# Early modulation: 27 of 64 weight chunks split into high and low parts, the other 37 left as they were

## The chip, the cores and the metric

One core of a Trainium2 chip runs the whole program. The metric is the device time of one execution in microseconds, from the first to the last instruction and what lies around them. Beside the timed runs there is one profiled execution, whose trace is what is read here.

## The reference

One layer of a streaming encoder runs over 512 prompt rows and 32 sample rows of width 2048. Two conditioning vectors (prompt and sample) give scales, shifts and gates for the rows:

```python
cs = jax.nn.silu(c)
mod = cs @ w_mod[li] + b_mod[li]              # w_mod is 2048 x 12288
sh_a, sc_a, gt_a, sh_f, sc_f, gt_f = [m[:, None, :] for m in jnp.split(mod, 6, axis=-1)]
h = rmsnorm(x, g_attn[li]) * (1.0 + sc_a) + sh_a
z = h @ w_in[li]
...                                           # two kinds of attention, w_out, a second norm
f, cnew = conv_ffn(h2, cstate, w_up[li], conv_w[li], conv_b[li], w_down[li])
```

Everything is float32. Before the first large product (`h @ w_in`) can run, the first third of `mod` must be known: the 4096 columns of `sh_a` and `sc_a`.

## The kernel before

**The early stage.** That first third is computed on TensorE with the two conditioning vectors as the stationary operand (two columns) and the weights of `w_mod` as the moving one. The weights come in 64 chunks, e0 to e63, of 128 partitions x 1024 values (512 KB). Eight chunks make a group (8 groups of 512 output columns); a chunk holds two blocks of 128 input rows by 512 columns, so there are two matmuls of 512 moving columns per chunk, in plain float32 (L1558). The profile shows each of them as two records.

**Buffers and the order of loads.** Four raw buffers `w_raw0` to `w_raw3` are filled in turn by one queue of DMAs that SyncE issues in the order of the list `STREAM` (L258, loop at L505). Chunk e goes to buffer e mod 4. Before each issue SyncE waits in `slot_free` until the chunk that lay four places earlier in the list is used up: for an early chunk that is `m_used`, TensorE's count of finished chunks. Since SyncE issues in order, a late buffer also holds back the ones behind it. Behind e61 stand two chunks of `w_in` (w0, w1), then e62 and e63.

**Around the chunks, in TensorE's own order (L1546 to L1580).** After e5 come eight small transposes of bias and norm rows (L1523; a first one stands at the very start), whose results VectorE copies to `cols` (L1108). Chunk e8 waits for these copies (`rows_ev`). After each of e8 to e23 come five transposes (L1575, L1576) that bring one slice of x, 128 columns of it, to its place; ScalarE squares and copies each slice (L835, L836), and VectorE adds the squares (L1196). After e28 follow two matmuls for the sum over partitions (L1533, L1534). After the second chunk of a group, the columns of the group before are turned from a row into partitions (`group_columns`, L1542). For that, ScalarE must have copied the group's row out of PSUM (`group_out`, L826), and for e33 this is `group_out(3)`. Two PSUM banks hold the groups in turn.

**ScalarE and VectorE** work through orders of their own, written out by hand (ScalarE L828 to L856, VectorE L1182 to L1219). After the sum of squares ScalarE takes a root (L801) and VectorE a reciprocal of 544 columns (L1205). Then, for each of 16 slices, VectorE multiplies (`h_mul`, L1168), ScalarE rounds the shifted slice to `x_hi` (`h_hi`, L817), and VectorE takes the rest as `x_lo` (`h_lo`, L1177); each does 512 columns and then 32. Slices 4q to 4q + 3 need groups 2q and 2q + 1. The first product of the attention part needs all 16 slices.

**Split products.** From `w_in` on, each weight chunk is split: ScalarE writes the part rounded to float32r to `w_hi` (L806), VectorE the rest to `w_lo` (L1149), each with four buffers, and TensorE forms three products of float32r operands for every float32 product (L1584 to L1586). The splits are counted in `s_hi` and `s_lo`, and `s_lo` frees the raw buffer.

## Time and profile before

| | |
|---|---|
| timed runs (3) | 2707.13, 2709.91, 2711.16 us; median 2709.91 us |
| the profiled execution's own time | 2706.82 us |
| its span, first to last instruction | 2705.0 us |
| mean granted clock of TensorE | 0.99 of 2.4 GHz |
| TensorE busy | 2619.0 us, 97% of the span |
| VectorE busy | 1634.6 us, 60% |
| ScalarE busy | 958.4 us, 35% |
| GpSimd busy | 524.9 us, 19% |
| DMA engines | 324.96 MB moved |

The busy share of an engine is a mean over stages that have different limits. The early stage is the first 155 us. Its product stage begins at 156 us, and everything behind it waits for that moment. A line name such as L1558 is a line of the kernel before; the changed kernel has its own line numbers.

### The profile page before, as it was taken

Reading aid. Unit: us, or ns where it says so; the run is one execution under the profiler, and the core shown is the slowest. Engines: PE = TensorE matmul, PEld = TensorE weight load, DVE = VectorE, ACT = ScalarE, POOL = GpSimd, SP = SyncE. Lnnn points to the kernel's source line nnn. Section 1 sums busy time; section 2 is a strip of 40 time slices with the busy share of each in tenths; the row PEclk is TensorE's granted clock in tenths of the full one; section 3 lists DMA queues with packets and bytes.
Section 4 is the critical chain, followed back from the end, with each engine's and each line's share of the span. In section 5 each row is a group of like instructions: output and inputs, shape, how many; then the busy total and the mean of one; then the engine's idle time right before and its main releaser. Section 6 shows DMA issues by size and latency. Waiting matters only on the chain.

```text
span 2705.0 us, 50278 instructions
## 1 busy us (share of the span) xinstructions
PE 2619.0 (97%) x19783; PEld 2448.8 (91%) x19783; DVE 1634.6 (60%) x3210; ACT 958.4 (35%) x1871; POOL 524.9 (19%) x461
## 2 busy tenths in 40 slices
PE   7999999999999999999999999999999999999997
PEld 2268889898988999899999999999999999999997
DVE  1469889874357888965554555555455555445554
ACT  2236666664344335422222222222222222222224
POOL 1057777761003452400000000000000000000003
PEclk9999999999999999999999999999999999999998
DMA  8886556562215654432332332233232223223231
GB/s 256 265 266 192 172 181 182 171 161 60 59 48 160 172 164 125 148 110 81 92 94 84 90 93 80 80 94 94 79 94 83 82 88 94 87 86 94 79 94 70
DMA packets 416210, 324.96 MB, mean 120 GB/s; under 512 B 44410, under 2 KB 360218, under 8 KB 414880
## 3 DMA queue, kind: packets, MB, share of 16 engines
q1 hardware_dynamic: 410032, 302.55, 37.6%
q0 software_dynamic: 5248, 14.56, 1.7%
q10 hardware_dynamic: 688, 4.47, 0.5%
q8 instruction: 169, 2.77, 0.4%
q14 instruction: 73, 0.60, 0.1%
HBM read 307.67 MB, written 14.07 MB: 119 GB/s over the span
## 4 chain that ended last, share of the span: by engine, by line
PE 84%; DVE 7%; DMA 3%; issue 2%; POOL 2%; ACT 1%; SPq 1%; ACTq 0%; DVEq 0%; POOLq 0%
PE ps L1584 25%; PE ps L1586 24%; PE ps L1585 24%; PE ps L1558 4%; DVE late_f L1256 3%; PE ps L1673 2%; PE ps L1639 2%; DMA w_raw<-in_w_out 2%; DMA w_raw<-in_w_mod 1%; PE ps L1657 1%; POOL oT L708 1%; DVE w_lo L1149 1%; SPq L547 1%; ACT w_hi L806 1%; PE ps L1595 1%
## 5 line engine op out<-in xcount | busy, mean ns | idle before, releaser
L1584 PE MATMUL ps<-x_hi,w_hi 128*128 128x272 f32 (+1 forms) x4480 | 1320.1, 295 | 32.1 <-DVE w_lo L1149 22.5
L1585 PE MATMUL ps<-x_lo,w_hi 128*128 128x272 f32 (+1 forms) x4480 | 1298.2, 290 | 0.0
L1586 PE MATMUL ps<-x_hi,w_lo 128*128 128x272 f32 (+1 forms) x4480 | 1296.2, 289 | 0.0
L1584 PEld LDWEIGHTS ps<-x_hi,w_hi 128*128 128x128 f32 x4480 | 850.3, 190 | 45.9 <-issue 27.6
L1586 PEld LDWEIGHTS ps<-x_hi,w_lo 128*128 128x128 f32 x4480 | 852.0, 190 | 0.0
L1585 PEld LDWEIGHTS ps<-x_lo,w_hi 128*128 128x128 f32 x4480 | 849.8, 190 | 0.0
L806 ACT ACTIVATE w_hi<-w_raw 128x1024 fp32r<-128x1024 f32 x368 | 375.0, 1052 | 1049.6 <-PE ps L1586 901.5
L1149 DVE TENSOR_TENSOR w_lo<-w_raw,w_hi 128x1024 fp32r<-128x1024 f32 x368 | 456.6, 1270 | 343.1 <-ACT w_hi L806 342.7
L1586 PE MATMUL ps<-y_hi,w_lo 128*128 128x272 f32 x1408 | 406.8, 289 | 0.0
L1584 PE MATMUL ps<-y_hi,w_hi 128*128 128x272 f32 x1408 | 406.1, 288 | 0.0
L1585 PE MATMUL ps<-y_lo,w_hi 128*128 128x272 f32 x1408 | 404.5, 287 | 0.0
L763 POOL TENSOR_TENSOR ext<-cv 128x544 f32<-128x544 f32 x1 | 1.5, 1509 | 1479.4 <-ACT cv L1056 1479.4
L1585 PEld LDWEIGHTS ps<-y_lo,w_hi 128*128 128x128 f32 x1408 | 265.3, 188 | 0.0
L1586 PEld LDWEIGHTS ps<-y_hi,w_lo 128*128 128x128 f32 x1408 | 264.7, 188 | 0.0
L1584 PEld LDWEIGHTS ps<-y_hi,w_hi 128*128 128x128 f32 x1408 | 264.6, 188 | 0.1
L1358 DVE SCALAR_TENSOR_TENSOR x<-ps,mod,x 128x272 f32<-128x272 f32 (+2 forms) x576 | 204.1, 399 | 69.8 <-PE ps L1586 69.8
L708 POOL TENSOR_TENSOR oT<-oT 128x512 f32<-128x512 f32 x150 | 223.7, 1492 | 33.7 <-ACT oT L870 25.7
L1415 DVE COPY u_shift<-ps 128x2 f32<-128x2 f32 x88 | 13.9, 158 | 307.4 <-PE ps L1586 307.4
L1256 DVE SCALAR_TENSOR_TENSOR oT<-w_raw,cs,oT 128x512 f32<-128x512 f32 x150 | 178.6, 1191 | 2.8
L708 POOL TENSOR_TENSOR late_f<-late_f 128x512 f32<-128x512 f32 x90 | 136.7, 1519 | 180.5 <-ACT late_f L870 175.8
L1558 PE MATMUL ps<-w_raw,cs 128*2 128x512 f32 x256 | 119.5, 614 | 13.8 <-DMA w_raw<-in_w_mod 13.1
L1256 DVE SCALAR_TENSOR_TENSOR late_f<-w_raw,cs,late_f 128x512 f32<-128x512 f32 x90 | 122.1, 1356 | 3.6 <-DMA w_raw<-in_w_mod 0.5
(195 smaller groups left out, 2095.8 us busy)
## 6 DMA issues: line engine op xcount, KB each, us to landing
w_raw<-in_w_mod SPq DMA_DIRECT2D x192, 512.0 KB, 4.6
w_raw<-in_w_up SPq DMA_DIRECT2D x176, 512.0 KB, 4.6
w_raw<-in_w_down SPq DMA_DIRECT2D x88, 512.0 KB, 4.2
w_raw<-in_w_in SPq DMA_DIRECT2D x56, 512.0 KB, 3.9
w_raw<-in_w_in SPq DMA_DIRECT2D x32, 256.0 KB, 3.7
w_raw<-in_w_out SPq DMA_DIRECT2D x16, 512.0 KB, 5.3
w_raw<-in_w_out SPq DMA_DIRECT2D x64, 128.0 KB, 3.9
x_transposed<-xT SPq DMA_DIRECT2D x4, 1088.0 KB, 8.6
```

The source lines that it names most:

```text
L547: sp.dma_start(dst[64 * u:64 * u + 64, 4 * m:4 * m + 4, :], src.rearrange("(i p) n -> p i n", p=64)).then_inc(ld_raw[slot], 16)
L708: ins = pool.tensor_tensor(acc, late_prod(n, 0) if p == 0 and k == 1 else acc, late_prod(n, k), ALU.add)
L806: act.activation(w_hi[c % NW][:, :], w_raw[raw][:, :], ACT.Copy).then_inc(s_hi, 1)
L1149: dve.tensor_tensor(w_lo[c % NW][:, :], w_raw[raw][:, :], w_hi[c % NW][:, :].bitcast(F32), ALU.subtract).then_inc(s_lo, 1)
L1256: ins = dve.scalar_tensor_tensor(out=acc_d(g), in0=w, scalar=c, in1=acc_d(g), op0=ALU.mult, op1=ALU.add)
L1358: ins = dve.scalar_tensor_tensor(out=x1[:, n, a:a + m], in0=b[:, a - HALF[h][0]:a - HALF[h][0] + m], scalar=mod[:, gate + n, g:g + 1], in1 ...
L1558: mm = pe.matmul(bank(7 - g % 2)[0:2, :], cs[:, kt, :], w_raw[raw][:, EG * k:EG * k + EG], start=kt == 0, stop=kt == KT - 1)
L1584: pe.matmul(out[:, 0:n], hi_w, hi_x, start=first, stop=False)
L1585: pe.matmul(out[:, 0:n], hi_w, lo_x, start=False, stop=False)
L1586: return pe.matmul(out[:, 0:n], lo_w, hi_x, start=False, stop=last)
L1639: mm = pe.matmul(S[t % 2][0:np_, pc:pc + n], zq[qi % 2][r, q0:q0 + np_], kk, start=True, stop=True)
L1673: mm = pe.matmul(B7[0:np_, oc:oc + vn], probsT[0:n, tc:tc + np_], v, start=first, stop=last)
```

## The change

- Chunks e7, e9, ..., e59 (27 of them, `SPLIT`) are split as the later weights are: ScalarE writes `w_hi`, VectorE writes `w_lo`, in the same four buffers, and TensorE multiplies both parts with a stationary operand of four columns. That operand is `c_parts`, which holds the high and the low parts of the two conditioning vectors. So a split chunk is four matmuls of 512 columns on float32r operands.
- The other 37 chunks stay plain float32, but their stationary operand `c_whole` has four columns too, two of them zero. A group's row is now four rows (high and low), and `group_columns` adds them up with a matmul against the small matrix `pair` instead of a transpose.
- SyncE waits for `s_lo` before it refills the buffer of a split chunk, and for `m_used` as before with the others.
- The orders of ScalarE and VectorE are written anew as loops over e. In step e each first splits chunk e + 3 (`AHEAD`), then does what stood there before. The work on the first twelve slices (`h_mul`, `h_hi`, `h_lo`) is tied to steps 31, 32, 36, 37, 52 and 53 (`H_AT`).
- All counts of `s_lo` behind the early stage are shifted by `ES`.

```diff
@@ -222,6 +222,11 @@
 SUM_AT = X_AT + KT + 4
 W_AT = 62
+SPLIT = range(7, 60, 2)
+ES = len(SPLIT)
+AHEAD = 3
+
+H_AT = {SUM_AT + 3: 0, SUM_AT + 4: 2, 36: 4, 37: 6, 52: 8, 53: 10}
@@ -299,7 +304,7 @@
-SC0 = FC0
+SC0 = ES + FC0
@@ -353,7 +358,10 @@
-        mod_rows = [on(st0, f"mod_rows{i}", [2, EG]) for i in range(2)]
+        mod_rows = [on(st0, f"mod_rows{i}", [4, EG]) for i in range(2)]
+        c_parts = on(st0, "c_parts", [P, KT, 4], F32R)
+        c_whole = on(st0, "c_whole", [P, KT, 4])
+        pair = on(st0, "pair", [P, 2])
@@ -494,7 +503,9 @@
                 if old[0] == "w":
-                    sp.wait_ge(s_lo, old[1] + 1)
+                    sp.wait_ge(s_lo, ES + old[1] + 1)
+                elif old[0] == "e" and old[1] in SPLIT:
+                    sp.wait_ge(s_lo, SPLIT.index(old[1]) + 1)
                 elif old[0] == "e":
                     sp.wait_ge(m_used, old[1] + 1)
@@ -598,6 +609,9 @@
+            pool.memset(c_whole[:, :, 2:4], 0.0).then_inc(consts, 1)
+            pool.wait_ge(consts, 5)
+            pool.tensor_tensor(pair[0:4, :], ident[0:4, 0:2], ident[0:4, 2:4], ALU.add).then_inc(consts, 1)
@@ -793,7 +807,10 @@
-            act.wait_ge(consts, 4)
+            act.wait_ge(cs_ok, 1)
+            act.activation(c_whole[:, :, 0:2], cs[:, :, :], ACT.Copy).then_inc(cs_ok, 1)
+            act.activation(c_parts[:, :, 0:2], cs[:, :, :], ACT.Copy).then_inc(c_hi, 1)
+            act.wait_ge(consts, 6)
@@ -808,6 +825,8 @@
             def hi_early(c):
                 if c >= NW:
                     act.wait_ge(g_done, 2 * ((c - NW) // 2) + 2)
+                elif c == 0:
+                    act.wait_ge(m_used, SPLIT[-1] + 1)
                 hi(c, RAW_OF[("w", c)] % NR, LOADED[("w", c)])
@@ -823,35 +842,42 @@
                 act.wait_ge(m_used, EPG * (g + 1))
                 if g >= 2:
                     act.wait_ge(e_t, g - 1)
-                act.activation(mod_rows[g % 2][:, :], bank(7 - g % 2)[0:2, :], ACT.Copy).then_inc(e_ev, 1)
-
-            for kt in range(KT):
-                if (X_AT + kt) % EPG == 0:
-                    group_out((X_AT + kt) // EPG - 1)
+                act.activation(mod_rows[g % 2][:, :], bank(7 - g % 2)[0:4, :], ACT.Copy).then_inc(e_ev, 1)
+
+            def hi_split(e):
+
+                n = SPLIT.index(e)
+                if n >= NW:
+                    act.wait_ge(m_used, SPLIT[n - NW] + 1)
+                hi(n, RAW_OF[("e", e)] % NR, LOADED[("e", e)])
+
+            def x_in(kt):
+
                 act.wait_ge(xt_t, kt + 1)
                 b = bank(2 * (kt % 2), 2)[:, 0:T]
                 if kt >= 2:
                     act.wait_ge(sq_add, max(1, kt - 2))
                 act.activation(n0_sq[kt % 2][:, :], b, ACT.Square).then_inc(sq_mul, 1)
                 act.activation(xT[:, kt, :], b, ACT.Copy).then_inc(xt_ev, 1)
-                if kt == 0:
+
+            for e in range(EC):
+                if e + AHEAD in SPLIT:
+                    hi_split(e + AHEAD)
+                if e % EPG == 1 and e > EPG:
+                    group_out(e // EPG - 1)
+                if 0 <= e - X_AT < KT:
+                    x_in(e - X_AT)
+                if e == X_AT + 1:
                     act.wait_ge(lam_dot, 2)
                     act.activation(tiny[:, 4:6], tiny[:, 6:8], ACT.Exp).then_inc(lam_exp, 1)
-            group_out(2)
-            root(0, n0_rstd[:, :])
-            for kt in range(EGT):
-                h_hi(kt)
-            group_out(3)
-            for kt in range(EGT, 2 * EGT):
-                h_hi(kt)
-            group_out(4)
-            group_out(5)
-            for kt in range(2 * EGT, 3 * EGT):
-                h_hi(kt)
-            group_out(6)
+                if e == SUM_AT + 1:
+                    root(0, n0_rstd[:, :])
+                if e in H_AT:
+                    h_hi(H_AT[e])
+                    h_hi(H_AT[e] + 1)
             hi_early(0)
             hi_early(1)
-            group_out(7)
+            group_out(E_GROUPS - 1)
             for kt in range(3 * EGT, KT):
                 h_hi(kt)
 
@@ -1179,47 +1205,65 @@
                                                    in1=x_hi[:, kt, a:a + c].bitcast(F32), op0=ALU.add, op1=ALU.subtract)
                 ins.then_inc(x_ok, 1)
 
-            dve.wait_ge(rows_t, len(ROW_COUNTS))
-            for i in range(1, len(ROW_COUNTS)):
-                row_out(i)
-            dve.wait_ge(ld_small, 80)
-            for i in range(2):
-                a, b = lam[2 * i], lam[2 * i + 1]
-                dve.tensor_tensor_reduce(a[:, :], a[:, :], b[:, :], 1.0, 0.0, ALU.mult, ALU.add,
-                                         tiny[:, 6 + i:7 + i]).then_inc(lam_dot, 1)
-            dve.wait_ge(rows_ev, len(ROW_COUNTS))
-            group_mod(0)
-            for kt in range(1, KT):
+            def lo_split(e):
+
+                n = SPLIT.index(e)
+                lo(n, RAW_OF[("e", e)] % NR, n)
+
+            def sum_row(kt):
+
                 dve.wait_ge(sq_mul, kt + 1)
                 if kt > 1:
                     dve.wait_ge(sq_add, kt - 1)
                 ins = dve.tensor_tensor(n0_acc[:, :], n0_sq[0][:, :] if kt == 1 else n0_acc[:, :],
                                         n0_sq[kt % 2][:, :], ALU.add)
                 ins.then_inc(sq_ok if kt == KT - 1 else sq_add, 1)
-            dve.wait_ge(lam_exp, 1)
-            step(dve.tensor_tensor(tiny[:, 3:4], tiny[:, 5:6], tiny[:, 4:5], ALU.subtract))
-            step(dve.tensor_scalar(neg_lam, tiny[:, 3:4], -LAMBDA_INIT, None, ALU.add))
-            group_mod(1)
-            group_mod(2)
-            dve.wait_ge(sd_ok, 1)
-            dve.reciprocal(n0_rstd[:, :], n0_rstd[:, :]).then_inc(rs_ok, 1)
-            dve.wait_ge(rs_ok, 1)
-            for q in range(4):
-                for g in range(max(3, 2 * q), 2 * q + 2):
-                    if g == E_GROUPS - 1:
-                        lo(0, RAW_OF[("w", 0)] % NR, 0)
-                        lo(1, RAW_OF[("w", 1)] % NR, 1)
-                    group_mod(g)
-                dve.wait_ge(mod_ok, q + 1)
-                for kt in range(EGT * q, EGT * q + EGT):
-                    h_mul(kt)
-                    if kt >= 2:
-                        h_lo(kt - 2)
-            h_lo(KT - 2)
-            h_lo(KT - 1)
+
+            dve.wait_ge(c_hi, 1)
+            dve.tensor_tensor(c_parts[:, :, 2:4], cs[:, :, :], c_parts[:, :, 0:2].bitcast(F32), ALU.subtract
+                              ).then_inc(c_lo, 1)
+            for e in range(EC):
+                if e + AHEAD in SPLIT:
+                    lo_split(e + AHEAD)
+                if e == 6:
+                    dve.wait_ge(rows_t, len(ROW_COUNTS))
+                    for i in range(1, len(ROW_COUNTS)):
+                        row_out(i)
+                    dve.wait_ge(ld_small, 80)
+                    for i in range(2):
+                        a, b = lam[2 * i], lam[2 * i + 1]
+                        dve.tensor_tensor_reduce(a[:, :], a[:, :], b[:, :], 1.0, 0.0, ALU.mult, ALU.add,
+                                                 tiny[:, 6 + i:7 + i]).then_inc(lam_dot, 1)
+                    dve.wait_ge(rows_ev, len(ROW_COUNTS))
+                if 1 <= e - X_AT < KT:
+                    sum_row(e - X_AT)
+                if e % EPG == 2 and e > EPG:
+                    group_mod(e // EPG - 1)
+                if e == SUM_AT + 2:
+                    dve.wait_ge(lam_exp, 1)
+                    step(dve.tensor_tensor(tiny[:, 3:4], tiny[:, 5:6], tiny[:, 4:5], ALU.subtract))
+                    step(dve.tensor_scalar(neg_lam, tiny[:, 3:4], -LAMBDA_INIT, None, ALU.add))
+                    dve.wait_ge(sd_ok, 1)
+                    dve.reciprocal(n0_rstd[:, :], n0_rstd[:, :]).then_inc(rs_ok, 1)
+                    dve.wait_ge(rs_ok, 1)
+                if e in H_AT:
+                    dve.wait_ge(mod_ok, H_AT[e] // EGT + 1)
+                    h_mul(H_AT[e])
+                    h_mul(H_AT[e] + 1)
+                if e - 1 in H_AT:
+                    h_lo(H_AT[e - 1])
+                    h_lo(H_AT[e - 1] + 1)
+            lo(0, RAW_OF[("w", 0)] % NR, ES)
+            lo(1, RAW_OF[("w", 1)] % NR, ES + 1)
+            group_mod(E_GROUPS - 1)
+            dve.wait_ge(mod_ok, KT // EGT)
+            for kt in range(3 * EGT, KT):
+                h_mul(kt)
+            for kt in range(3 * EGT, KT):
+                h_lo(kt)
 
             def lo_early(c):
-                lo(c, RAW_OF[("w", c)] % NR, c)
+                lo(c, RAW_OF[("w", c)] % NR, ES + c)
...
@@ -1539,8 +1583,8 @@
                 if g:
                     pe.wait_ge(e_tev, g)
                 for t in range(EGT):
-                    mm = pe.transpose(bank(5)[:, 2 * t:2 * t + 2], mod_rows[g % 2][0:2, P * t:P * t + P],
-                                      ident[0:2, 0:2])
+                    mm = pe.matmul(bank(5)[:, 2 * t:2 * t + 2], mod_rows[g % 2][0:4, P * t:P * t + P], pair[0:4, :],
+                                   start=True, stop=True)
                 mm.then_inc(e_t, 1)
 
             for e in range(EC):
@@ -1548,15 +1592,26 @@
                 if first and g >= 2:
                     pe.wait_ge(e_ev, g - 1)
                 if e == 0:
-                    pe.wait_ge(cs_ok, 1)
+                    pe.wait_ge(cs_ok, 2)
                 if e == EPG:
                     pe.wait_ge(rows_ev, len(ROW_COUNTS))
                 raw = RAW_OF[("e", e)] % NR
-                pe.wait_ge(ld_raw[raw], LOADED[("e", e)])
+                if e in SPLIT:
+                    pe.wait_ge(c_lo, 1)
+                    pe.wait_ge(s_lo, SPLIT.index(e) + 1)
+                else:
+                    pe.wait_ge(ld_raw[raw], LOADED[("e", e)])
                 for k in range(EK):
                     kt = EK * (e % EPG) + k
-                    mm = pe.matmul(bank(7 - g % 2)[0:2, :], cs[:, kt, :], w_raw[raw][:, EG * k:EG * k + EG],
-                                   start=kt == 0, stop=kt == KT - 1)
+                    if e in SPLIT:
+                        n = SPLIT.index(e) % NW
+                        pe.matmul(bank(7 - g % 2)[0:4, :], c_parts[:, kt, :], w_hi[n][:, EG * k:EG * k + EG],
+                                  start=kt == 0, stop=False)
+                        mm = pe.matmul(bank(7 - g % 2)[0:4, :], c_parts[:, kt, :], w_lo[n][:, EG * k:EG * k + EG],
+                                       start=False, stop=kt == KT - 1)
+                    else:
+                        mm = pe.matmul(bank(7 - g % 2)[0:4, :], c_whole[:, kt, :], w_raw[raw][:, EG * k:EG * k + EG],
+                                       start=kt == 0, stop=kt == KT - 1)
                 mm.then_inc(m_used, 1)
                 if e == 5:
                     pe.wait_ge(ld_rows, 16 * 10)
```

The same moves as they stand in the engines' own orders, at three places. `lo` of chunk e is the instruction that writes `w_lo`, `hi` the one that writes `w_hi`.

VectorE at the start of the program, before the change: the nine copies to `cols` are the first work.

```order
L1108 COPY cols<-ps 128x32 [waits rows_t]
L1108 COPY cols<-ps 128x96 [waits rows_t]
L1108 COPY cols<-ps 128x48 [waits rows_t]
L1108 COPY cols<-ps 128x88 [waits rows_t] x6
L1188 ISA lambda,tiny<-lambda 128x64 [waits ld_small]
L1188 ISA tiny 128x1
```

VectorE at the same place, changed:

```order
L1134 COPY cols<-ps 128x32 [waits rows_t]
L1223 TENSOR_TENSOR c_parts<-cs,c_parts 128x16x2 [waits c_hi]
L1175 TENSOR_TENSOR w_lo0<-w_raw3,w_hi0 128x1024 [waits s_hi]
L1175 TENSOR_TENSOR w_lo1<-w_raw1,w_hi1 128x1024 [waits s_hi]
L1134 COPY cols<-ps 128x96 [waits rows_t]
L1134 COPY cols<-ps 128x48 [waits rows_t]
L1134 COPY cols<-ps 128x88 [waits rows_t] x6
```

The `lo` of e7 (from `w_raw3`) and of e9 (from `w_raw1`) now stand ahead of eight of the nine copies for which e8 waits.

ScalarE from the root to `group_out(3)`, the copy to `mod_rows`, before the change:

```order
L801 ACTIVATE n_rstd<-ps,tiny 128x544 [waits ss_ok]
L817 ACTIVATE x_hi<-hT,mod 128x512 [waits n_mul]
L817 ACTIVATE x_hi<-hT,mod 128x32
L817 ACTIVATE x_hi<-hT,mod 128x512 [waits n_mul]
L817 ACTIVATE x_hi<-hT,mod 128x32
L817 ACTIVATE x_hi<-hT,mod 128x512 [waits n_mul]
L817 ACTIVATE x_hi<-hT,mod 128x32
L817 ACTIVATE x_hi<-hT,mod 128x512 [waits n_mul]
L817 ACTIVATE x_hi<-hT,mod 128x32
L826 ACTIVATE mod_rows<-ps 2x512 [waits e_t,m_used]
```

ScalarE at the same place, changed (root, `hi` of e33, two slices, `hi` of e35, two slices, `group_out(3)`):

```order
L818 ACTIVATE n_rstd<-ps,tiny 128x544 [waits ss_ok]
L823 ACTIVATE w_hi<-w_raw 128x1024 [waits ld_raw1,m_used]
L836 ACTIVATE x_hi<-hT,mod 128x512 [waits n_mul]
L836 ACTIVATE x_hi<-hT,mod 128x32
L836 ACTIVATE x_hi<-hT,mod 128x512 [waits n_mul]
L836 ACTIVATE x_hi<-hT,mod 128x32
L823 ACTIVATE w_hi<-w_raw 128x1024 [waits ld_raw3,m_used]
L836 ACTIVATE x_hi<-hT,mod 128x512 [waits n_mul]
L836 ACTIVATE x_hi<-hT,mod 128x32
L836 ACTIVATE x_hi<-hT,mod 128x512 [waits n_mul]
L836 ACTIVATE x_hi<-hT,mod 128x32
L845 ACTIVATE mod_rows<-ps 4x512 [waits e_t,m_used]
```

Two splits now stand between the root and `group_out(3)`, the second one in the middle of the four slices.

VectorE from the reciprocal on, before the change (`h_mul` is L1168):

```order
L1158 TENSOR_TENSOR mod<-ps,cols 128x4 [waits e_t]
L1158 TENSOR_TENSOR mod<-ps,cols 128x4
L1205 RECIPROCAL n_rstd<-n_rstd 128x544 [waits sd_ok]
L1168 SCALAR_TENSOR_TENSOR hT<-xT,mod,n_rstd 128x512 [waits mod_ok,rs_ok]
L1168 SCALAR_TENSOR_TENSOR hT<-xT,mod,n_rstd 128x32
L1168 SCALAR_TENSOR_TENSOR hT<-xT,mod,n_rstd 128x512
L1168 SCALAR_TENSOR_TENSOR hT<-xT,mod,n_rstd 128x32
L1168 SCALAR_TENSOR_TENSOR hT<-xT,mod,n_rstd 128x512
```

VectorE at the same place, changed (`h_mul` is L1194; the rows begin behind the `lo` of e33):

```order
L1244 TENSOR_TENSOR tiny<-tiny 128x1 [waits lam_exp]
L1245 TENSOR_SCALAR tiny<-tiny 128x1 [waits dve_own]
L1247 RECIPROCAL n_rstd<-n_rstd 128x544 [waits sd_ok,dve_own]
L1194 SCALAR_TENSOR_TENSOR hT<-xT,mod,n_rstd 128x512 [waits mod_ok,rs_ok]
L1194 SCALAR_TENSOR_TENSOR hT<-xT,mod,n_rstd 128x32
L1194 SCALAR_TENSOR_TENSOR hT<-xT,mod,n_rstd 128x512
L1194 SCALAR_TENSOR_TENSOR hT<-xT,mod,n_rstd 128x32
L1175 TENSOR_TENSOR w_lo<-w_raw,w_hi 128x1024 [waits s_hi]
L1194 SCALAR_TENSOR_TENSOR hT<-xT,mod,n_rstd 128x512 [waits mod_ok]
L1194 SCALAR_TENSOR_TENSOR hT<-xT,mod,n_rstd 128x32
L1194 SCALAR_TENSOR_TENSOR hT<-xT,mod,n_rstd 128x512
L1194 SCALAR_TENSOR_TENSOR hT<-xT,mod,n_rstd 128x32
```

The reciprocal now stands behind the `lo` of e33, and the `lo` of e35 between the first two and the next two slices.

## Rows read from the trace of the kernel before

**Rows 1.** Chain of waits, first 260 us: start us, length us, what

```profile
30.43 1.03 PE ps L1523 x8
31.46 5.24 PE ps L1558 x12
36.70 0.59 PE ps L1575 x4
...
42.17 0.59 PE ps L1575 x4
42.76 0.17 PE ps L1576
42.93 1.81 PE ps L1558 x4
...
85.77 1.06 PE ps L1533 x2
...
87.75 3.56 DVE n_rstd L1205
...
97.05 0.40 PE ps L1542 x4
97.45 13.82 PE ps L1558 x32
...
145.35 4.61 DMA w_raw<-in_w_mod
150.00 5.16 PE ps L1558 x8
```

**Rows 2.** Stretches: TensorE busy, its weight loads, VectorE, ScalarE, GpSimd, clock, DMA

```profile
18.00:21.00 3.00, 0.00 (x0) 0.00 (x0) 0.00 (x0) 0.00 (x0) 0.00 (x0) 0.84 1.00 330
105.00:110.00 5.00, 5.00 (x13) 1.02 (x12) 0.00 (x0) 0.59 (x1) 0.00 (x0) 1.00 0.90 304
149.00:152.00 3.00, 2.00 (x3) 0.34 (x4) 1.32 (x2) 0.44 (x1) 0.00 (x0) 0.62 0.83 277
180.00:200.00 20.00, 20.00 (x160) 19.72 (x158) 19.86 (x15) 10.26 (x14) 18.25 (x11) 1.00 0.79 255
```

**Rows 3.** Timeline, 146 to 150 us, ScalarE, VectorE and SyncE

```profile
146.78 1.06 ACT L806 ACTIVATE w_hi<-w_raw 128x1024 fp32r<-128x1024 f32 x1 [9.99 <-DMA w_raw<-in_w_in]
147.87 1.22 DVE L1149 TENSOR_TENSOR w_lo<-w_raw,w_hi 128x1024 fp32r<-128x1024 f32 x1 [7.53 <-ACT w_hi L806]
149.12 0.37 SPq L529 DMA_DIRECT2D w_raw<-in_w_in  x1
```

**Rows 4.** Loads issued from 98 to 110 us, issue to landing

```profile
DMA to landing us min/median/max: 3.7/4.5/4.8
```

**Rows 5.** Loads issued from 50 to 64 us, issue to landing

```profile
DMA to landing us min/median/max: 4.2/4.3/4.4
```

**Rows 6.** Groups by shape, first 245 us: busy us, mean ns, idle before

```profile
L1168 DVE SCALAR_TENSOR_TENSOR hT<-xT,mod,n_rstd 128x512 f32<-128x512 f32 x16 | 12.0, 747 | 0.1
L1177 DVE SCALAR_TENSOR_TENSOR x_lo<-hT,mod,x_hi 128x512 fp32r<-128x512 f32 x16 | 11.9, 746 | 0.0
L817 ACT ACTIVATE x_hi<-hT,mod 128x512 fp32r<-128x512 f32 x16 | 11.5, 721 | 20.3 <-DVE hT L1168 20.3
L835 ACT ACTIVATE n_sq<-ps 128x544 f32<-128x544 f32 x16 | 10.0, 624 | 22.0 <-PE ps L1576 22.0
L836 ACT ACTIVATE xT<-ps 128x544 f32<-128x544 f32 x16 | 9.9, 618 | 0.0
L826 ACT ACTIVATE mod_rows<-ps 2x512 f32<-2x512 f32 x8 | 4.6, 581 | 54.5 <-PE ps L1558 54.5
```

**Rows 7.** Timelines: VectorE at 31 and 91 us, ScalarE at 92 us

```profile
31.50 1.30 DVE L1108 COPY cols<-ps 128x96 f32<-128x96 f32 x8 [26.02 <-PE ps L1523]
...
91.33 2.57 DVE L1168 SCALAR_TENSOR_TENSOR hT<-xT,mod,n_rstd 128x512 f32<-128x512 f32 x6
...
92.28 2.58 ACT L817 ACTIVATE x_hi<-hT,mod 128x512 fp32r<-128x512 f32 x6 [4.57 <-DVE hT L1168]
```

5 lines of the change are left out of this document (3 added, 2 removed).

## The prediction

> **What bounds the kernel now.** I first took the stretches of the early stage, then the chain of waits through it, then the loads. The chain lies on TensorE from 30 us to 155 us almost without a gap: eight whole chunks take 13.82 us, 1.73 us each [rows 1]. One slice of x adds 0.59 + 0.17 = 0.76 us of transposes, so a chunk with a slice takes 1.81 + 0.76 = 2.57 us [rows 1]. So TensorE sets the pace. But it is a close race: at that pace the DMA engines are busy 90% of the time at 304 GB/s [rows 2], and a load needs 4.5 us (3.7 to 4.8) from issue to landing [rows 4]. A buffer comes round every 4 x 1.73 = 6.9 us, of which load and matmuls take 4.7 + 1.73 = 6.4. The slack per buffer is half a microsecond. Whatever makes a buffer wait longer than that takes the bound away from TensorE.
>
> **Cost of a chunk on TensorE.** A whole chunk stays at 1.73. No row has a float32r operand with four stationary columns. The nearest: 160 products of 272 columns in 20.00 us, 0.125 us each [rows 2], which scaled by columns is 0.235 us for 512; half a record of the plain chunk (13.82 / 32 / 2) is 0.216 [rows 1]. Four of them are 0.86 to 0.94; I take 0.90. Each split chunk saves 0.83 us, 27 save 22.4 us of TensorE's time. If the four cost as much as the plain records (1.73), all of that is gone.
>
> **Cost of a split on the buffer.** A split takes 1.06 us on ScalarE, then 1.22 on VectorE, and SyncE issues again 0.03 us after it (146.78 + 1.06 + 0.03 + 1.22 = 149.09, issue at 149.12) [rows 3]. From landing to a free buffer that is 2.36 us against 1.73 before. With a load of 4.7 the buffer's round is 7.1 us, 1.77 per chunk: no faster than before, if nothing else stands in its way. Things do. TensorE takes the next whole chunk only after the split one, so the refill of the whole one's buffer comes 0.90 + 1.73 = 2.63 us after the `lo`, and the refill of the next split buffer is queued behind it in SyncE's order and lands behind it in the DMA queue. From one `lo` over this path to the `lo` three pairs later: 0.03 + 2.63 + 0.03 + load 4.7 + spacing of the two landings s + 2.36 = 9.75 + s for six chunks. s lies between 0.3 (two loads together, no row) and 1.56 (1.73 x 0.90, the queue full). That gives 1.68 to 1.88 per chunk; the other round holds it at 1.77 at least, the column matmuls add 0.05. I take 1.87.
>
> **Stage by stage**, in time of the profiled execution, + is later.
>
> 1. To the end of e8: +3.5. e8 waits for the copies to `cols`, and these now stand behind the `lo` of e7 and e9 on VectorE. e9 is issued when e5 is done at 30.4 [rows 1], lands 4.3 later at 34.7 [rows 5], + 1.06 + 1.22 and the gaps gives 37.1, + 1.30 for the copies [rows 7] gives 38.4, and e8 ends at 40.2 instead of at 36.7 [rows 1]. (The new small steps at the very start, four copies and a sum of four rows, are hidden: TensorE has nothing to do from 18 to 21 us for want of loads [rows 2].)
> 2. e9 to e23: -6.6 for eight split chunks x 0.83. But the order on ScalarE gives back 3.5 (2 to 5): `group_out` and two 0.62 us passes per slice [rows 6] now share it with the splits, and the columns at e9 and e17 wait for a `group_out` behind a split that waits for its load. Net -3.1.
> 3. e24 to e28: -0.5. Two split chunks could save 1.7, the buffer round allows 0.5.
> 4. End of e28 to start of e34: +8.3. Before: 97.45 - 85.77 = 11.7 [rows 1]. This stretch ends with a real wait of TensorE, for `group_out(3)` behind four `h_hi`. Now the chain is: refill of e32's and e33's buffers 0.5, load of e33 4.9, `hi` and `lo` 2.4, small steps 0.2, reciprocal 3.6 [rows 1], first `h_mul` 0.83 of a pair (2.57 / 3 = 0.86 a slice [rows 7]), second slice and its `h_hi` 1.7 [rows 6, 7], `hi` of e35 1.05, its `lo` 1.25, `h_mul` 0.83, `h_hi` of two slices 1.7, `group_out` 0.6 [rows 6], columns 0.4 [rows 1]: 20.0. TensorE stands still for some 10 us, all four buffers full and no load running. What was 8.3 us of chain more can't be hidden by chunks that take less time.
> 5. e34 to e63: +4.2. Before: 155.2 - 97.4 = 57.7 [rows 1]. Now four chunks stand ready, 2 x 2.63 = 5.3. The other 26 x 1.87 = 48.6. After the splits of e39 and e55 VectorE has three pairs of `h_mul` or `h_lo` (about 1.66 a pair, 0.83 a slice) before the next `lo`, 5.0 where 2 x 1.87 - 1.22 = 2.5 are free: 2 x 2.4 = 4.8. Then w0 and w1 take two places of the queue ahead of e62: 3.2. Sum 61.9.
> 6. The clock: +3.2. In the trace of before the stretch 149 to 152 us shows 0.62 granted [rows 2], behind the wait of TensorE for the load of e62 (issued at 145.35, there at 149.96 [rows 1]): the clock had fallen from 2.4 to 1.2 GHz, and the last two chunks took 5.16 instead of 3.46 [rows 1]. That 1.7 us is in the 57.7 of before, not in my 61.9, and will come again. The standstill of step 4 costs the same once more, 1.5.
>
> The last four slices are as long as before: eight steps of 0.83 on VectorE behind the last columns. From there on the program is the same and is only shifted. Sum: 3.5 - 3.1 - 0.5 + 8.3 + 4.2 + 3.2 = **+15.6 us**. The profiled execution took 2706.8, so 2722.4; the median of the timed runs is 3.1 above it, so **2725.5 us**.
>
> **Bounds.** Step 2 gives back 2 to 5; in step 4 the load is 3.7 to 5.5 (7 to 9); step 5 with 1.77 to 1.93 a chunk and 2 to 7 for VectorE (-5 to +4); the clock 0 to 5. Not all ends fall together: +8 to +24.
>
> **Rivals.**
>
> - *The clock falls all through e34 to e63.* TensorE works 2.63 of 3.74 us per pair there, with a hole of 1.1 before each split chunk. For it: the wait for e62 took the clock down [rows 2]. Against: these holes are shorter. At 1.2 GHz 2.63 becomes 5.26, the path over six chunks 12.4 + s, 2.2 to 2.3 a chunk: +10, so 2735. The Trainium skill ("TensorE: Matmul & The Clock Gate", section "HAM oscillation") says that groups of matmuls with waits for loads between them throttle the array again and again. By that rule this case is the likelier one; the trace here agrees for a long hole and has no series of short ones. Chance 0.17.
> - *Faster.* The orders don't bind: ScalarE and VectorE, 35% and 60% busy over the span, do their splits in the holes, and the saving on TensorE comes through up to the DMA engines' limit. The place is step 4: if `group_out(3)` comes no later than e33, its +8.3 is 0 and the four buffers never stand full. With 1.56 to 1.7 a chunk behind it (DMA at its limit, 30 chunks x 0.1) steps 1 to 5 are 3.5 - 6.6 - 0.5 - 3 = -7: 2703. It decides as soon as the chain from e28 is under 11.7 us; with a reciprocal behind the `lo` of e33 I find no way. Chance 0.06.
> - *No change.* Steps 1 and 2 cancel, and the wait of step 4 is half as long, caught up by 26 chunks at 1.77 less a shorter load of 3.7 when the queue is empty [rows 4]. 2710. Chance 0.07.
> - *The four matmuls of a split chunk cost 1.73.* Nothing is saved in step 2 (+6.6, less what the waits hide): some +21, 2731. Against: the products of rows 2 run at one column a cycle. Chance 0.05.
>
> **Chances.** The forecast 0.65, with 2718 to 2733 as its own range; the rivals as above. I give 2716 to 2738. About 0.2% (5.4 us) is what a measurement can tell from no change here. Slower: 0.65 + 0.17 + 0.05 = 0.87; same 0.07; faster 0.06.
>
> **What would show it.** The first `h_mul` pair near 96 us as before's 91, TensorE without work for 8 to 12 us before the columns in the middle of e33 to e34, ended by the copy to `mod_rows`, itself behind `x_hi`. The copies to `cols` from 37 us and not 31.5. The first product at 170 us or later instead of 156. SyncE's waits moved from TensorE to VectorE's `w_lo`. DMA share in the second half of the early stage below 0.90. Everything behind the first product as long as before. I am wrong if the columns before e34 wait for less than 3 us, or if the first product comes before 160 us.

## The result, and the profile after

The changed kernel takes 2759.8 us (2752.5 to 2760.2, 4 runs) against 2710.2 of the kernel before beside it: ratio 1.018, 95% interval 1.0164 to 1.0196. Slower, as forecast, but by 49.6 us instead of 15.6, and outside the range. The profiled execution has a span of 2758.4 us against 2705.0: 53.4 us to explain.

I follow these through the program by marks (differences are taken before rounding). Behind the early stage they are the first product of the attention stage, the first copy to `u_shift` (the FFN's first chunk) and the last one (the end of the FFN loop).

| us | before | after | difference |
|---|---|---|---|
| end of e8 | 36.7 | 43.1 | +6.4 |
| end of e28 | 85.8 | 94.5 | +8.8 |
| start of e34 | 97.4 | 115.9 | +18.5 |
| end of e63 | 155.2 | 189.3 | +34.1 |
| first product | 156.2 | 190.95 | +34.8 |
| first copy to `u_shift` | 1059.2 | 1097.3 | +38.1 |
| last copy to `u_shift` | 2615.0 | 2668.4 | +53.4 |

The forecast had +15.6 at the fifth line and nothing more behind it. The 3.3 us between the first product and the first copy to `u_shift` are within scatter: over all kernels of this study, which are the same program there, that stretch takes 899.4 to 909.5 us.

The first view of after is the chain of waits, 30 to 200 us: start us, length us, what. It answers [rows 1].

```profile
38.14 1.31 DVE cols L1134 x8
39.50 3.58 PE ps L1613 x4
...
99.83 1.07 ACT w_hi L823
100.92 1.22 DVE w_lo L1175
102.44 3.56 DVE n_rstd L1247
106.02 0.93 DVE hT L1194 x2
106.97 1.76 ACT x_hi L836 x4
108.73 0.96 ACT w_hi L823
109.71 1.23 DVE w_lo L1175
110.94 0.84 DVE hT L1194 x2
111.80 0.94 ACT x_hi L836 x3
112.73 0.52 issue
113.56 0.48 ACT mod_rows L845
114.09 1.86 PE ps L1586 x8
115.95 3.52 PE ps L1613 x4
119.90 4.87 DMA w_raw<-in_w_mod
124.86 1.07 ACT w_hi L823
125.94 1.23 DVE w_lo L1175
127.17 0.84 DVE hT L1194 x2
128.03 3.42 ACT x_hi L836 x8
131.45 0.96 ACT w_hi L823
132.43 1.24 DVE w_lo L1175
133.80 0.58 PE ps L1608
```

Where [rows 1] have one unbroken piece of 13.82 us of TensorE, a single chunk of TensorE here stands between chains over the DMA engines, ScalarE and VectorE. Two pieces are to be read closely. The line L1586 is the columns of a group: 1.86 us, where [rows 1] have 0.40. And e34 (L1613 at 115.95) takes 3.52 us for four records, which is TensorE at 1.2 GHz instead of 2.4.

The second view is the stretches of after (us, TensorE busy, its granted clock, DMA share, GB/s) in 20 us pieces; the clock of before was 1.00 from 80 to 140 us and 0.91 from 140 to 180.

```profile
80.00:100.00 20.00, 18.02 (x60) 0.91 0.73 224
100.00:120.00 20.00, 8.65 (x22) 0.66 0.30 102
120.00:140.00 20.00, 14.45 (x39) 0.84 0.67 210
...
160.00:180.00 20.00, 14.53 (x39) 0.83 0.61 199
```

And the stretch e34 to e63 as a whole, after:

```profile
115.90:189.30 73.40, 55.41 (x145) 0.88 0.67 211
```

and before:

```profile
97.40:155.20 57.80, 54.78 (x133) 0.97 0.87 284
```

The loads move some 210 GB/s, where [rows 2] show 304. Neither TensorE nor the DMA engines are the bound any more. The third view says who is (TensorE's waits, 20 to 200 us: us in total, times, longest):

```profile
PE ps L1586 <- ACT mod_rows L845: 17.2, 6, 10.7
PE ps L1608 <- DVE w_lo L1175: 14.1, 8, 3.6
PE ps L1613 <- DMA w_raw<-in_w_mod: 10.5, 3, 7.9
PE ps L1613 <- DVE cols L1134: 4.6, 1, 4.6
```

In the same stretch of before the first of these was 2.1 us, the second did not exist, and the third, 10.3 us, was there already.

SyncE's own waits, 100 to 190 us, show why the loads slow down. After, and below it before:

```profile
SPq L527 <- PE ps L1613: 54.3, 15, 16.9
```

```profile
SPq L516 <- PE ps L1558: 34.3, 25, 1.8
```

The buffer that SyncE waits for is mostly that of a whole chunk, which TensorE takes only after the split chunk before it. The longest of these waits, 16.9 us, spans the standstill before e34.

The fourth is a place at which I had not looked, the head of the FFN loop (timeline of TensorE). Before:

```profile
1457.63 0.39 PE L1584 MATMUL ps<-x_hi,w_hi 128*128 128x272 f32 x1 [1.56 <-issue]
```

After:

```profile
1495.99 0.39 PE L1639 MATMUL ps<-x_hi,w_hi 128*128 128x272 f32 x1 [1.60 <-issue]
...
1498.78 0.39 PE L1641 MATMUL ps<-x_hi,w_lo 128*128 128x272 f32 x1 [1.51 <-issue]
1498.97 0.43 PE L1639 MATMUL ps<-x_hi,w_hi 128*128 128x272 f32 x1
```

TensorE stands still once at each jump back to the head of the loop in the kernel before. In the changed one it runs eight matmuls and stands still a second time, and the matmuls behind take 0.43 instead of 0.29 us: the clock has fallen (granted clock 0.50 from 1498.9 to 1502.2 us; before, 1.00 from 1457.7 to 1461.0). This happens at all four heads, in code that the change doesn't touch.

### The profile page after: what moved, and what is told of

It is laid out like the page before. It is cut to its first block, busy times and chain, and to the rows that moved or that the text cites. A ratio compares the mean times of both kernels' runs of the same rounds, so it can differ in the third digit from the quotient of the medians.

```text
span 2758.4 us, 50452 instructions
## 1 busy us (share of the span) xinstructions
PE 2629.9 (95%) x19815; PEld 2465.1 (89%) x19815; DVE 1663.6 (60%) x3238; ACT 985.0 (36%) x1900; POOL 525.7 (19%) x463
## 4 chain that ended last, share of the span: by engine, by line
PE 79%; DVE 7%; DMA 5%; issue 3%; ACT 2%; POOL 2%; SPq 1%; ACTq 0%; DVEq 0%; POOLq 0%
PE ps L1639 24%; PE ps L1641 23%; PE ps L1640 23%; DVE late_f L1300 3%; DMA w_raw<-in_w_mod 2%; PE ps L1728 2%; PE ps L1694 2%; DMA w_raw<-in_w_out 2%; PE ps L1613 2%; ACT w_hi L823 1%; POOL oT L722 1%; DVE w_lo L1175 1%; PE ps L1712 1%; SPq L558 1%; DVE oT L1300 1%
## 5 line engine op out<-in xcount | busy, mean ns | idle before, releaser
L823 ACT ACTIVATE w_hi<-w_raw 128x1024 fp32r<-128x1024 f32 x395 | 403.9, 1054 | 1154.0 <-PE ps L1641 923.1
L1175 DVE TENSOR_TENSOR w_lo<-w_raw,w_hi 128x1024 fp32r<-128x1024 f32 x395 | 487.5, 1261 | 451.4 <-ACT w_hi L823 450.8
L1066 ACT ACTIVATE y_hi<-cv 128x512 fp32r<-128x512 f32 x88 | 33.1, 424 | 228.6 <-DVE cv L1517 228.6
```

The lines of the kernel that those rows point to most:

```text
L823: act.activation(w_hi[c % NW][:, :], w_raw[raw][:, :], ACT.Copy).then_inc(s_hi, 1)
L1066: ins = act.activation(y_hi[par][:, jj, a:a + n], cv[1][:, a + 2 * g:a + 2 * g + n], ACT.Copy)
L1175: dve.tensor_tensor(w_lo[c % NW][:, :], w_raw[raw][:, :], w_hi[c % NW][:, :].bitcast(F32), ALU.subtract).then_inc(s_lo, 1)
```

## The experiments

Four theories. **A**: ScalarE and VectorE do their work in the order in which it is written, and the new order puts work that TensorE waits for behind splits whose loads have not landed. **B**: the clock that falls in these waits is a large part of the loss. **C**: the columns of a group as matmuls with `pair`. **D**: the place of the FFN loop in TensorE's stream of instructions. The changed kernel has 91 instructions more ahead of it. "First product" is read from the profile of each kernel. "Loop" is the time from the first to the last copy to `u_shift`: 1555.8 us before, 1571.1 after.

**pad_before.** The kernel before with 91 instructions more ahead of the loop:

```diff
                 mm.then_inc(m_used, 1)
+                if e == 1:
+                    for _ in range(22):
+                        pe.matmul(bank(2)[:, 0:2], ones[:, :], ident[:, 0:2], start=True, stop=True)
+                    for _ in range(5):
+                        pe.wait_ge(consts, 4)
```

> The kernel before, with 22 tiny float32 matmuls (128x2, into a bank that nothing reads yet) and 5 more waits that are already met, placed behind e1, so that as many instructions more stand ahead of the FFN loop on TensorE as the changed kernel has (91), and nothing else is changed. Theory D (the 15.3 us that the changed kernel loses inside the untouched FFN loop come from where the loop lies in TensorE's instruction stream: a second standstill of 1.5 to 2.0 us some 2.8 us behind each of the four loop heads, and the lower clock after it): the stretch from the first to the last sum over the loop (u_shift first to last) grows from 1555.8 to about 1571 us, second standstills appear at the four loop heads, and the time is about 2725 us (+15, early stage within 1 us). Rival (the loss follows from what the early stage does to loads or buffers, or from the clock's history, not from the position): the loop stays at 1555.8 us with one standstill a head, and the time at 2710 to 2712 us.

Measured: 2723.5 us (2722.9 to 2724.5) against 2707.9, ratio 1.0059 (1.0042 to 1.0076). The early stage did not move (first product 155.7), the loop took 1568.3, and the second standstills are there:

```profile
1461.06 0.39 PE L1589 MATMUL ps<-x_hi,w_hi 128*128 128x272 f32 x1 [1.74 <-issue]
...
1464.12 0.39 PE L1591 MATMUL ps<-x_hi,w_lo 128*128 128x272 f32 x1 [1.79 <-issue]
```

So 91 instructions that compute nothing made the kernel 15.6 us slower. In the profiled execution 12.5 us are in the loop and 3.7 in the attention stage, within its scatter. That is as much as my whole forecast, from a cause that was not in it.

**after_pad.** The changed kernel with one such matmul and one met wait (5 instructions).

> The changed kernel, with one tiny float32 matmul and one met wait more behind e1, which moves the FFN loop by 5 instructions on TensorE. In the kernel before 32 instructions ran from the loop head on without a second standstill; in the changed one TensorE stops after the 20th (nine weight loads, eight matmuls and what stands ahead of them). Theory D: instructions come in pieces of 16, and what counts is how far into a piece the loop head lies; moved by 5 it lies at the start of one, as in the kernel before, so the second standstills at the four heads go, the loop takes about 1556 us instead of 1571.1, and the time is about 2745 us (15 less than 2760) with the first product still at 198 us. Rival (history of loads or clock): no change, 2758 to 2761 us, second standstills still there.

Missed: 2760.7 us (2757.9 to 2763.6), the loop 1574.8. The second standstills did not go, they came five instructions sooner, behind six matmuls instead of eight. That gave the second form of the theory: not the distance from the head counts, but a fixed place in the stream, at instruction 16080.

**after_pad24.** The changed kernel with six such matmuls (24 instructions), so that the head lies behind that place.

> The changed kernel with six tiny float32 matmuls behind e1: the FFN loop lies 24 instructions later. In the changed kernel the second standstill behind a loop head came after 21 instructions, with the loop moved by 5 it came 5 instructions earlier: at the same absolute place, number 16080 of TensorE's stream. The kernel with columns by transposes, 64 instructions earlier, had none. Moved by 24 the head lies 3 behind that end: no second standstills, the loop at about 1556 us, the time at about 2745 us, the early stage as in the changed kernel (last group's columns at 190 us). Rival (any moving changes the loop at random, or history): 2758 to 2762.

Measured: 2747.3 us (2741.3 to 2748.8), ratio 1.0145 (1.0128 to 1.0162); loop 1556.7, one standstill a head; first product 189.4. 12.5 us less than the changed kernel, for more instructions.

**pad_before_far, pad_before_256, pad_before_512.** The kernel before with 54, 86 and 150 matmuls instead of 22, which puts the head 128, 256 and 512 further than in `pad_before`.

> The kernel before with 54 tiny float32 matmuls and 5 met waits behind e1: the loop lies 219 instructions later, at 16187, which is 128 more than in pad_before (16059, 2723.5 us). Theory D with pieces of 128 instructions: again a head 21 ahead of an end, second standstills at the four heads, loop at 1568 to 1571 us, time 2723 to 2728 (up to 3 us of it from the added matmuls). Rival (the place 16080 is a single one, not a period): loop at 1556 us, one standstill a head, time 2709 to 2713.

> The kernel before with 86 tiny float32 matmuls and 5 met waits behind e1: the FFN loop lies at 16315, 256 more than in pad_before. The early stage will be some 18 us later and says nothing; only the loop is read. If the place repeats every 256 instructions: second standstills at the four heads and 1567 to 1572 us from the first to the last u_shift. If it repeats at longer distance or not at all: 1555 to 1558 us, one standstill a head.

> The same with 150 matmuls and 5 waits: the loop lies at 16571, 512 more than in pad_before, the early stage some 35 us later. If the place repeats every 256 or 512: second standstills, 1567 to 1572 us in the loop. If not: 1555 to 1558 us.

Measured: far 2720.1 us (2717.5 to 2722.9), 256 2756.6 and 512 2777.1 (one run each). The totals hold the filling, which delays the first product by 11.3, 27 and 52 us, more than I had expected (3, 18 and 35); the loops are what counts: 1557.3, 1572.0, 1572.3 us. So the period of 128 falls and one of 256 stands. The heads of `pad_before_512`:

```profile
1512.84 0.39 PE L1589 MATMUL ps<-x_hi,w_hi 128*128 128x272 f32 x1 [1.80 <-issue]
...
1515.63 0.29 PE L1591 MATMUL ps<-x_hi,w_lo 128*128 128x272 f32 x1 [1.52 <-issue]
```

All kernels of this study give one table. Distance is counted in instructions from the loop's head to the next place at 16080 or a multiple of 256 from it.

| distance | kernels | loop, us | second standstill, us |
|---|---|---|---|
| 16 | after_pad | 1574.8 | 1.8 to 2.1, all four heads |
| 21 | after, after_ahead2, after_hspread, pad_before, _256, _512 | 1566.8 to 1572.3 | 0.8 to 2.1, all four heads |
| 34 | split_late | 1560.8 | 0.6 to 0.9, three heads of four |
| 47, 48 | split_one, ghost | 1556.1, 1556.3 | none |
| 85 to 253 | before and the nine others | 1554.4 to 1560.2 | none (in pad_before_far one first standstill of 3.27) |

The 1560.2 us are those of x_only; the next highest is 1557.3. Behind two of its four single standstills (1.81 and 1.75 us) the clock fell: 0.57 from 1457.0 to 1461.0 us.

What is fetched there shows in the DMA rows. Queue q8 of after, over the whole run, and in three stretches around the first head (packets, MB, share):

```profile
q8 instruction: 169, 2.77, 0.4%
```

```profile
q8 instruction: 1, 0.02, 4.8%
...
q8 instruction: 1, 0.02, 10.7%
...
q8 instruction: 1, 0.02, 5.0%
```

They move 16.4 KB each. The three begin between 1492.5 and 1494.1, between 1496.0 and 1496.6 and between 1498.8 and 1500.0, with none between these. The share of the second, 10.7% of 16 engines for 0.6 us, makes it 1.03 us long. So the second piece starts only when the first instructions behind the jump run (from 1495.99), and TensorE goes on at 1498.78. In the kernel before it is the same: head at 1457.63, the next piece between 1457.7 and 1459. There 112 instructions stand ahead of the place, and nothing waits. From the first matmul behind the jump to the end of a second standstill it is 2.5 to 3.3 us in all kernels that have one. At 0.063 us an instruction (0.125 a matmul with its weight load) 21 instructions cover 1.3 us of that, 34 cover 2.1, and 47 cover 3.0. The period of 256 and the standstill at each jump agree. It calls the crossing of a boundary mostly hidden; here it is hidden from 47 instructions on.

The stages of the early part stand in one table. The sum of squares starts at the end of e28; the columns of group 3 are in the second column.

| kernel | end of e28 | from there to e34 | e34 to e63 | of it TensorE idle | first product |
|---|---|---|---|---|---|
| before | 85.8 | 11.6 | 57.8 | 3.0 | 156.2 |
| after | 94.5 | 21.4 | 73.4 | 17.9 | 190.95 |
| after_pad | 91.9 | 21.7 | 75.6 | 16.3 | 190.9 |
| after_pad24 | 90.2 | 21.7 | 75.9 | 16.3 | 189.4 |
| after_cols | 89.6 | 20.4 | 70.6 | 15.6 | 181.7 |
| after_ahead2 | 91.8 | 17.2 | 73.5 | 16.1 | 184.2 |
| after_hspread | 95.5 | 11.9 | 76.9 | 17.7 | 185.95 |
| split_one | 88.7 | 11.6 | 63.1 | 5.0 | 165.0 |
| split_late | 88.1 | 23.5 | 77.5 | 16.8 | 190.8 |
| after_fill | 90.2 | 21.7 | 74.1 | 9.5 | 187.7 |
| ghost | 98.9 | 23.4 | 76.8 | 11.5 | 200.7 |
| full_best | 87.2 | 11.2 | 70.8 | 15.7 | 170.2 |
| full_out | 79.3 | 12.2 | 68.2 | 16.0 | 160.7 |
| x_only | 87.0 | 10.9 | 56.7 | 3.2 | 155.6 |
| x_out | 81.2 | 10.9 | 60.2 | 3.8 | 153.3 |
| x_more | 80.1 | 10.9 | 58.4 | 3.4 | 150.4 |

after, after_pad and after_pad24 are the same program here but for one and six tiny matmuls: 4 us in a stage and 1.6 in the first product is what single profiles scatter. So are x_only, x_out and x_more from e34 on: 56.7 to 60.2 us, at granted clocks of 1.00, 0.94 and 0.97.

**after_cols.** The changed kernel with the columns by transposes, as before, and the sum of the high and low parts on VectorE:

```diff
-                    mm = pe.matmul(bank(5)[:, 2 * t:2 * t + 2], mod_rows[g % 2][0:4, P * t:P * t + P], pair[0:4, :],
-                                   start=True, stop=True)
+                    mm = pe.transpose(bank(5)[:, 4 * t:4 * t + 4], mod_rows[g % 2][0:4, P * t:P * t + P],
+                                      ident[0:4, 0:4])
```

> The changed kernel, but the columns of each group are made by four transposes of 4 rows (as before with 2 rows) instead of four plain float32 matmuls with the pair matrix, and VectorE adds the high and low columns (two small operations of about 0.07 to 0.15 us more in each group). Theory C (the columns by matmul cost 1.05 us a group at full clock and 1.86 at half clock against 0.34 for transposes): 8 groups give back 0.7 to 1.5 us each where TensorE is what is waited for, so 4 to 8 us of the 33 in the early stage: first product ready at 190 to 194 us instead of 198.3, time 2752 to 2756. Rival A (the early stage is bound by the chain split - buffer - chunk over ScalarE and VectorE, in which the columns only fill a wait): less than 2 us, 2758 to 2761. Theory D says of this kernel that the loop head, 64 instructions (four times 16) earlier, lies as in the changed kernel: second standstills at the four heads stay, and the loop stays at about 1571 us.

Measured: 2733.95 us (2731.4 to 2736.2), ratio 1.0099 (1.0082 to 1.0116); first product 181.7, so 9.3 us from the columns, above the 4 to 8 of theory C. (The 198.3 us of the expectation are another mark, the product that waits for the last slice of h; by that mark it is 189.5 here.) The loop took 1556.2: the head is 64 instructions earlier, and the loop does not behave as in the changed kernel. That sentence of the expectation was wrong, since it took a period of 16. The groups by shape, first 200 us (busy us, mean ns, idle before). After:

```profile
L1586 PE MATMUL ps<-pair,mod_rows 4*128 4x2 f32 x64 | 10.8, 287 | 17.2 <-ACT mod_rows L845 17.2
```

after_cols:

```profile
L1589 PE MATMUL ps<-ident,mod_rows 4*128 4x4 f32 x32 | 3.8, 220 | 16.5 <-ACT mod_rows L845 16.5
```

Each float32 matmul is two records, each transpose one. 7.0 us less TensorE work gave 9.3, or 7.7 against after_pad24, whose early stage is the changed kernel's too.

**after_ahead2.** `AHEAD = 2` in place of 3.

> The changed kernel with AHEAD = 2: each split is issued two chunks ahead of its use in the hand-written orders instead of three, so that it stands behind one chunk's other work more (copies out, slices of x, columns) and the other work stands behind one split fewer. Theory A (the orders written by hand on ScalarE and VectorE are what the early stage loses in, the split's copy and subtraction holding up x slices, copies out and columns): the early stage changes by several us in one direction, my own sum of the waits says 4 to 8 us better, first product at about 191 to 194 us. Rival B (the loss is the clock that falls in TensorE's waits) and C (columns): the first product moves by less than 2 us, unless the half-clock stretches go with the waits.

Measured: 2746.8 us (one run), first product 184.2: 6.7 us earlier, as theory A says. The gain lies ahead of e34; the stretch behind it stays at 73.5. e8 ends at 36.6, as in the kernel before, so the order (`AHEAD`) is the whole of the 6.4 us there. But e28 ends at 91.9, no earlier than in after_pad: the delay at e8 was mostly caught up by then anyway. The rest of the gain is the stretch to e34, 17.2 us.

**after_hspread.** `H_AT = {35: 0, 39: 2, 43: 4, 47: 6, 51: 8, 55: 10}`.

> The changed kernel with the slices of h moved in the hand-written orders: pairs of slices at e = 35, 39, 43, 47, 51, 55 instead of 31, 32, 36, 37, 52, 53. Theory A (ScalarE and VectorE, in order, hold the copy out of group 3 and later splits behind slices of h): the 10.7 us in front of the columns of group 3 shrink to under 3, the standstills of 3.6 us behind the paired slices go, the loads that waited for the freed buffers go out earlier, and the first product comes 8 to 14 us earlier (177 to 183 instead of 191 us). Rival B (the clock, or the load pace of 1.7 us a chunk, takes the time back): the standstill goes, but the first product moves by less than 4 us. The loop head is not moved: loop at 1571 us.

Measured: 2750.3 us (one run), first product 185.95. The standstill before the columns of group 3 went from 10.7 to 2.2 us:

```profile
106.40 0.82 PE L1586 MATMUL ps<-pair,mod_rows 4*128 4x2 f32 x6 [2.18 <-ACT mod_rows L845]
```

but the columns of groups 4, 5 and 6 now waited 2.9 us each. The stretch to e34 is 9.5 us shorter, but only 5.0 us came through, below theory A's range and above the rival's; the stretch e34 to e63 took 3.5 us more.

**split_one.** `SPLIT = range(59, 60)`: the new orders and columns, one split.

> The changed kernel with SPLIT = range(59, 60): one chunk is split, the new orders on ScalarE and VectorE, the products of four rows and the columns by matmul stay. If the orders and the columns alone cost the early stage (theories A and C), the first product comes at 172 to 180 us; if it is the splits and the buffers that they hold (their copy and subtraction ahead of other work, buffers freed by VectorE), at 158 to 166 us, that is 2 to 10 us behind the kernel before. My sum: standstill at group 3 of about 7 us instead of 10.7, columns 8 x 0.7, cols copies no longer behind a split: 166 to 172. Its loop head lies 47 instructions ahead of an end of a piece of 128: theory D expects no or a short second standstill there.

Measured: 2716.6 us (one run), first product 165.0, loop 1556.1. That is in the range for the splits, just under my own sum. So orders and columns cost 8.8 us, the other 26 splits 26 us: 5.8 up to e28, 9.8 from there to e34, 10.3 behind e34.

**split_late.** `SPLIT = range(33, 60, 2)`.

> The changed kernel with the 14 odd chunks from e33 to e59 split and those before unsplit. Theory A (the loss lies from e24 on, where the ring of four loads sets the pace and each split puts 2.4 us of copy and subtraction between landing and product): the group 3 columns stand at about 102 to 108 us, e34 to e63 take 70 to 74 us as in the changed kernel, first product at 174 to 181 us. Rival (each split costs the same, about 1 us, wherever it stands): 165 + 13 = 178, with the stretch behind e34 at about 67 and the columns of group 3 at 108. So it is the stretch e34 to e63 that tells them apart: over 70 or under 68. Its loop head lies 34 instructions ahead of an end of a piece of 128: between 21 (second standstill) and 47 (none); theory D makes a short one of under 1 us or none.

Measured: 2748.95 us (one run), first product 190.8, that of the changed kernel, and above my range. Thirteen splits fewer gave 2 to 6 us up to e28, and they were lost again behind it: the columns of group 3 stood at 109.8 behind the full standstill of 10.7, and e34 to e63 took 77.5. So the stretch test says over 70, theory A's side. The splits behind e33 alone make the early stage as late as all 27 do: the 13 early ones neither gain nor cost anything in this order, within the scatter of single profiles. On the loop its short second standstills are what theory D had said.

**after_fill.** Matmuls without effect in the waits:

```diff
+            def fill(n, b):
+                for _ in range(n):
+                    pe.matmul(bank(b)[:, 0:P], ones[:, :], ident[:, :], start=True, stop=True)
...
+                    fill({1: 4, 2: 4, 3: 4, 4: 24}.get(g, 0), 4)
                     group_columns(g - 1)
```

and 11 before the wait of e8, 5 to 9 before those of e37, e39, e45, e53 and e55.

> The changed kernel with tiny-effect matmuls (ones x ident, 128x128 float32, into a bank that nobody reads) in the places where TensorE stands still in the early stage: 24 before the columns of group 3, 11 before the wait for the row copies at e8, 4 each before the columns of groups 0 to 2, 5 to 9 before the waits of e37, e39, e45, e53, e55. Theory B (the clock that falls to half in these waits is a large part of the loss): the half-clock stretches behind them go and the first product comes 5 to 10 us earlier than 191. Rival A (what is lost is what the other engines make TensorE wait for, the clock only stretches work that hides in it): less than 3 us, either sign, though the granted clock rises. Its loop head lies 85 ahead of an end of a piece: theory D expects one standstill a head and the loop at 1556 us.

Measured: 2738.8 us (one run), loop 1555.3, first product 187.7, 1.7 to 3.2 us earlier than in after_pad24 and the changed kernel. The granted clock over 20 to 150 us rose from 0.84 to 0.91. The 24 matmuls lasted 5.5 us at a granted clock of 1.00 and left 5.35 of the wait before group 3's columns unfilled. The columns behind it still took 1.86 us, so the clock was held only in part. TensorE's idle time behind e34 fell from 17.9 to 9.5 us by the filling, and the stretch took no less. Theory B as a large part falls for what was filled; what a clock of 1.00 would give wasn't measured.

**ghost.** ScalarE and VectorE split as in the changed kernel; TensorE takes every chunk unsplit, and a slot is freed when both are done:

```diff
-                if e in SPLIT:
-                    pe.wait_ge(c_lo, 1)
-                    pe.wait_ge(s_lo, SPLIT.index(e) + 1)
-                else:
-                    pe.wait_ge(ld_raw[raw], LOADED[("e", e)])
+                pe.wait_ge(ld_raw[raw], LOADED[("e", e)])
```

> The changed kernel in which ScalarE and VectorE split the 27 chunks as before, but TensorE takes all 64 chunks unsplit from the loaded tile (c_whole), and a slot of a split chunk is freed when both its product and its subtraction are done. So no product waits for a subtraction. Theory A1 (the in-order streams: the copy out, the x slices and the slices of h stand behind splits whose loads have not landed): the loss stays, first product at 186 to 194 us. Theory A2 (the 2.4 us of copy and subtraction between landing and product in a ring of four loads): the waits at the split products go and TensorE works 0.8 us longer for each; first product at 165 to 174 us.

Measured: 2749.05 us (one run), first product 200.7, loop 1556.3. The products wait for no subtraction, and it got worse by 10 us, above both ranges. TensorE's waits there, 20 to 200 us:

```profile
PE ps L1587 <- ACT mod_rows L846: 23.2, 7, 11.6
```

So taking away the waits for the subtraction is not enough in this order: the copy out of each group, on ScalarE behind a split whose load has not landed, is waited for in their place (17.2 us in after). That speaks for A1. How much of the 10 us is A1 stays open, since ghost also gives TensorE back 27 x 0.8 = 22 us of work, less what its waits hide. The clean test of A1 is `full_out` below. That the other (A2) would bind once the order is mended, ghost doesn't exclude.

**full_best.** The changed kernel with all three: transposes, `AHEAD = 2`, spread slices.

> All 27 splits with the three repairs together: columns by transposes (-9.2 us in the first product alone), AHEAD = 2 (-6.7 alone), slices of h spread over e35 to e55 (-5.0 alone). If they are independent: 191 - 21 = 170 us, time about 2722; if AHEAD = 2 and the spread slices remove the same wait: 173 to 177 us, time 2725 to 2730. Theory of the ring (every split adds latency from landing to product, whatever the orders): not under 165 us, so slower than before in any case. Loop head 85 ahead of an end: loop at 1556 us.

Measured: 2721.45 us (2718.5 to 2726.2), ratio 1.0052 (1.0037 to 1.0068); first product 170.2 and time as for independent gains, to a microsecond.

**full_out.** The same, with the copy out ahead of the split in ScalarE's order:

```diff
+                if e % EPG == 1 and e > EPG:
+                    group_out(e // EPG - 1)
                 if e + AHEAD in SPLIT:
                     hi_split(e + AHEAD)
-                if e % EPG == 1 and e > EPG:
-                    group_out(e // EPG - 1)
```

> full_best with one change: in ScalarE's order the copy out of a group stands ahead of the split of the same step, not behind it. In full_best TensorE stood 1.6 to 2.9 us before the columns of groups 0, 1, 2, 4, 5, 6 (12.7 us in all), since ScalarE waited there for the landing of the load two chunks on. Theory A1: these waits shrink to under 1 us each and the first product comes 7 to 11 us earlier, 159 to 163 instead of 170 us, time 2710 to 2714. Rival (ring of loads: what TensorE does not wait at the columns it waits for at the next split product): the first product moves by less than 3 us, and the waits for w_lo grow from 8.6 us.

Measured: 2711.0 us (2707.6 to 2715.1) against 2708.0, ratio 1.0012 (1.0003 to 1.0021); first product 160.7. Two lines changed places and 9.5 us came back, of them 7.9 up to e28: theory A1, within its range. With all 27 splits in place 30.2 of the 34.8 us of the early stage are gone. But behind e34 it is still 68.2 us, 10.4 more than before, and TensorE idles 16.0 there. Its waits now, 20 to 200 us:

```profile
PE ps L1611 <- DVE w_lo L1175: 12.2, 11, 2.8
PE ps L1616 <- DMA w_raw<-in_w_mod: 10.9, 3, 7.4
PE ps L1589 <- ACT mod_rows L845: 7.1, 5, 1.9
```

The waits at the columns fell from 13.4 to 7.1 us, those for `w_lo` rose from 8.6 to 12.2. So the rival has a part: behind e34 what TensorE doesn't wait for at the columns it waits for, in part, at the next split.

**x_only, x_out, x_more.** Splits where TensorE is the bound: transposes, `AHEAD = 2`, the old `H_AT`, and `SPLIT = range(11, 24, 2)`; x_out also has the copy out first, and x_more has `range(9, 28, 2)` on top.

> The changed kernel with columns by four transposes (and the addition on VectorE), AHEAD = 2, and only the seven odd chunks from e11 to e23 split, which lie in the stretch of the x slices, where TensorE of before had no wait and the loads had room (DMA share 0.69). Theory A (a split pays where TensorE is what is waited for and costs where the loads and the other engines are): seven times 0.8 us less TensorE work, less what the four rows, the columns (8 x 0.07) and the later orders cost (split_one lost about 3 us there beside its columns): first product at 152 to 158 us against 156.2 of before, time 2704 to 2710 us against 2708. Rival (any split costs about 1 us, as 26 splits cost 26 us between split_one and the changed kernel): 164 to 168 us and 2716 to 2720. Loop head 105 instructions ahead of an end: theory D expects the loop at 1556 us.

> x_only with the same change of order (the copy out ahead of the split). It removes the waits of 1.6 us before the columns of groups 0 and 1. Theory A1: first product at 152 to 154 us instead of 155.6, time 2699 to 2703 against 2708 of the kernel before, so the faster of all. Rival: the x stretch takes it back, no change against x_only (2704).

> x_out with the ten odd chunks from e9 to e27 split instead of the seven from e11 to e23. Theory A (a split pays in the stretch in which TensorE is what is waited for, which ends about where the x slices end): e9 and the stretch e25 to e27 give under 1 us each, since the loads set the pace there: first product at 151 to 154 us, time 2697 to 2701 (x_out 2699.5). Rival (each split placed there is worth 0.8 us as in the x stretch): 2.5 us better, first product at 150.5 to 151.2. Third: the split of e9 ahead of the copies of the rows to columns costs 2 us on e8: 155.

Both x_only and x_out came out in the ranges of theory A.

| kernel | time, us | ratio to before | first product | last x transpose |
|---|---|---|---|---|
| x_only | 2704.1 (2700.4 to 2709.0) | 0.9986 (0.9977 to 0.9995) | 155.6 | 77.7 |
| x_out | 2699.45 (2697.0 to 2703.4) | 0.9967 (0.9955 to 0.9978) | 153.3 | 71.9 |
| x_more | 2700.5 (2697.9 to 2706.1) | 0.9971 (0.9961 to 0.9981) | 150.4 | 71.2 |

x_out is faster than both kernels, by 8.5 us (0.3%) than the one before. The splits alone didn't do it: in x_only e28 ends at 87.0, later than before, and with the copy out first at 81.2. No run has the order of x_out without any split, so the 8.5 us aren't divided between the two. Its chain of waits (start us, length us, what) is TensorE's again behind e33, in pieces as in [rows 1]:

```profile
87.80 3.41 ACT x_hi L836 x8
91.21 0.48 ACT mod_rows L845
92.15 13.83 PE ps L1616 x32
106.31 13.83 PE ps L1616 x32
```

x_more's early stage is 3 us shorter still, where its rival had put it. But only 1.1 us of that lie up to e28; 1.8 lie from e34 on, where the two kernels are the same program. So the first product doesn't tell theory A from the rival, and over nine runs the time equals that of x_out.

## Why the forecast failed, step by step

The forecast's own test was met (columns before e34 wait 10.7 us, first product behind 170), and its direction held. Of the 37.8 us between 15.6 and 53.4, 15.3 lie in the loop, 8.9 up to e28, 1.4 from there to e34, 8.2 behind e34 (11.4 more than step 5 had, less the 3.2 of step 6); the remaining 4 are the scatter of the attention stage and the last columns. Three statements of the forecast failed, and one sum.

**"Everything behind the first product as long as before" failed: +15.3 us.** I took untouched code for unchanged time. `pad_before` shows 12.5 us of it in the kernel before, for 91 instructions alone; the six kernels with this distance lie 11.0 to 16.5 us above the 1555.8. What the second standstills themselves take is 7.2 us in after. The rest goes with the clock, which was down for 3.4 to 6.8 us behind each of the four.

**"The column matmuls add 0.05" failed: 7.7 to 9.3 us.** I had priced a float32 matmul of 4x128 by two columns with the transposes' 0.40 of [rows 1]. It is two records instead of one a transpose, 1.05 us a group and 1.86 where the clock is down, on the path of most of the eight groups. `after_cols` shows it (against after_pad24 and after). It sits in steps 2 to 5.

**Step 5 failed: e34 to e63 took 73.4 us, not 61.9.** I had the pace from the round of buffers, 1.87 a chunk, and ScalarE had no part in it. Of the 11.5 us, about 3 are the columns (`after_cols`, 70.6; within the scatter of a stage), and 2.6 the copy out behind a split that waits for its load (`full_best` to `full_out`). For the rest I have no experiment. The chain shows where to look: four slices of h, 3.42 us on ScalarE at 128.03, stand ahead of the split at 131.45, its product starts at 133.80, and the whole chunk behind it frees its buffer only at 140.7, where the next load goes out. With every order mended, the 13 splits there still make it 68.2 us, with waits at `w_lo` in the rows, where x_only and x_out without them take 56.7 and 60.2. Whether these are the round of four buffers, longer than I had it, or slices of h ahead of splits, stays open. (The lower bound of the spacing s, 0.3 us, came from no row. In after two loads issued at 119.5 and 119.9 landed at 123.5 and 124.8, 1.3 us apart.)

**Steps 1 to 3 failed by their sum: +8.8 instead of -0.1** (+4.4 to +8.8 over after, after_pad and after_pad24). The saving on TensorE comes through once the order is mended, and the order ate it: `full_out` has e28's end at 79.3 and `x_out` at 81.2, against 85.8 before and 94.5 after. Between these two and after lie 13 to 15 us. About 2 of them are the columns, the rest is the order and, in x_out, the splits left out at e7 and e9; I had allowed 2 to 5 for it. The copy out ahead of the split is worth 7.9 us of it (`full_best` to `full_out`) and 5.8 (`x_only` to `x_out`).

Step by step:

1. To the end of e8, forecast +3.5: measured +6.4. The mechanism was right (copies to `cols` at 38.14, forecast 37.1). `after_ahead2`, in which the split of e9 stands behind the copies, has e8's end back at 36.6. What I missed is that e8 itself ran with the clock down, 3.58 instead of 1.73 us.
2. and 3. e9 to e28, forecast -3.6: measured +2.4, with the dear columns of three groups (2 us) in it.
4. e28 to e34, forecast +8.3 (20.0 us): measured +9.7 (21.4). The chain came as written: copy and subtraction of a load, reciprocal, pairs of slices, copy out; the last 1.4 us are the columns and the clock in them. It was a matter of where the slices stand, not of the splits: `after_hspread` has 11.9.
5. As above.
6. The clock, forecast +3.2: the mean granted clock from 20 to 190 us fell from 0.96 to 0.86. It is spread over six places. The 1.7 us behind the wait for e62, which I had said would come again, did not: the last two chunks took 1.88 us each. `after_fill` gave 1.7 to 3.2 us for raising it part of the way; how much the rest is worth stays open.

The four matmuls of a split chunk were priced right: L1608 and L1610 start 0.23 us apart, 0.92 a chunk against 0.90 forecast. A rival stood on that price; none stood on the places that failed.

Of the rivals, "the clock falls all through e34 to e63" was nearest to the measured time (2735) and not the cause: the clock was 0.88 there. It was down in three pieces, behind waits of 10.7, 3.6 and 3.6 us; the waits of 1.9 us left it at 2.4 GHz.

That the orders don't bind ("faster") was not so here: faster is only the kernel with the orders mended and the splits kept to the x stretch.

The sum in the profiled executions: 8.8 (orders and columns, `split_one`), 26 (26 splits), 3.3 (attention stage, within its scatter) and 15.3 (loop) make 53.4.

## What to carry to other kernels

Instructions added anywhere ahead of a loop move its head: before a small change is judged, look at the first fifty instructions behind each jump back for a second "issue" gap, and compare with a version that is moved by some ten instructions. Where an engine works in the written order, put what another engine waits for ahead of what itself waits for a load: that swap of two lines gave 9.5 us. And take time off an engine only in the stretch where it is the bound: with seven splits there and the mended order the kernel is 8.5 us faster, with all 27 the best order still lost 3.

## What the runs showed of the hardware

- Behind the jump of a loop of TensorE the first matmul starts 1.3 to 2.0 us late (once 3.27). If the head lies 16 or 21 instructions ahead of a multiple of 256 from a fixed place, a second standstill of up to 2.1 us follows, at 34 of up to 0.9, from 47 on none.
- Two standstills of 1.5 us with 1.3 us of matmuls between them were enough to bring the clock from 2.4 to 1.2 GHz behind them (0.43 instead of 0.29 us a matmul) at all four heads of after, but at only two of four in after_ahead2 and after_hspread. The single ones of before (1.56 to 1.74 us) were not enough, two of the four in x_only (1.81 and 1.75) were. So it isn't settled by the length of a standstill alone.
- The same wait for the load of e62 brought the clock down in before (3.0 us) and in x_out (3.1), and not in pad_before (3.0) nor in x_only (2.7).
- A float32 matmul of a 4x128 tile by two columns is two records at 0.131 us, a transpose of the same tile one at about 0.10.
- The same program section, the attention stage, took 899.4 to 909.5 us in different kernels. A difference within that range in single profiles says nothing.
